# Second block's input sent to the channels unnormalised, its two norms computed beside the projections

## The reference, cut to what matters

```python
return rmsnorm(x, g_final)            # end of the first block
...
h = _rms_norm(x, g_pre_mix[l])        # start of the second
proj = h @ w_in[l]
qa, ka, va, c_q, c_kv, k_r, gate_logits = _split_cols(
    proj, [MOBA_WIDTH, MOBA_WIDTH, MOBA_WIDTH, MLA_Q_LORA, MLA_KV_LORA, MLA_ROPE, 2 * D_MODEL])
...
gates = jax.nn.sigmoid((gate_logits + b_gate[l]).astype(jnp.float32)).astype(x.dtype)
merged = gates[..., :D_MODEL] * o_a + gates[..., D_MODEL:] * o_b
x = x + _rms_norm(merged @ w_out[l], g_post_mix[l])
```

## Time and profile before

| | us |
|---|---|
| median of 3 runs | 913.61 |
| lowest, highest | 911.22, 915.33 |
| profiled execution, its own time | 917.53 |
| span of that execution | 915.7 |
| PE busy | 852.1 (93%) |
| DVE busy | 419.4 (46%) |
| ACT busy | 417.5 (46%) |
| POOL busy | 410.0 (45%) |

### The profile page before, as it was taken

One profiled execution on the slowest core, in us unless ns is written; L12 is line 12 of the kernel. 1 busy time (PEld: TensorE's weight loads), 2 busy tenths in 40 slices (PEclk: granted clock), 3 DMA queues, 4 the chain that ended last, 5 costly groups with the idle time before them and its releaser, 6 DMA issues.

```text
span 915.7 us, 14674 instructions
## 1 busy us (share of the span) xinstructions
PE 852.1 (93%) x5699; PEld 739.3 (81%) x5699; DVE 419.4 (46%) x647; ACT 417.5 (46%) x648; POOL 410.0 (45%) x197
## 2 busy tenths in 40 slices
PE   5899999979889799999999799999998799999996
PEld 3578877856567699999997687899897699999995
DVE  3556468893522623323425414544355644243334
ACT  4435313333644434444444474565754544444443
POOL 2444000000036165565563687655555455646643
PEclk9899999999899989999999999999999999999999
DMA  9674564127324256556553377444344155665651
GB/s 322 206 273 135 201 218 161 47 68 244 103 92 138 69 165 194 191 178 191 181 186 104 117 217 171 138 117 119 124 150 161 47 185 183 185 186 190 193 162 46
DMA packets 93821, 145.55 MB, mean 159 GB/s; under 512 B 15435, under 2 KB 63792, under 8 KB 93776
## 3 DMA queue, kind: packets, MB, share of 16 engines
q1 hardware_dynamic: 92896, 143.23, 50.6%
q0 software_dynamic: 848, 1.70, 0.7%
q10 hardware_dynamic: 32, 0.01, 0.0%
HBM read 143.87 MB, written 1.05 MB: 158 GB/s over the span
## 4 chain that ended last, share of the span: by engine, by line
PE 73%; DVE 12%; issue 6%; ACT 4%; POOL 3%; DMA 1%; SPq 0%; DVEq 0%; ACTq 0%; POOLq 0%
PE bank L1608 71%; POOL w_lo L592 2%; ACT w_hi L647 2%; POOL z_lo L621 1%; PE bank L1876 1%; PE bank L1693 1%; DVE h_f L1154 1%; DVE hg_kb L1246 1%; DVE hg_kf L1246 1%; DMA raw<-in_w_in 1%; DMA x<-in_x 1%; DVE w_lo L1092 1%; PE bank L2172 1%; DVE x L1564 1%; DVE merged L1530 1%
## 5 line engine op out<-in xcount | busy, mean ns | idle before, releaser
L592 POOL TENSOR_TENSOR w_lo<-raw,w_hi 128x1024 fp32r<-128x1024 f32 (+2 forms) x161 | 389.3, 2435 | 472.7 <-ACT w_hi L647 451.7
L647 ACT ACTIVATE w_hi<-raw 128x1024 fp32r<-128x1024 f32 (+1 forms) x218 | 225.8, 1044 | 226.6 <-PE bank L1608 191.9
L1092 DVE TENSOR_TENSOR w_lo<-raw,w_hi 128x1024 fp32r<-128x1024 f32 x60 | 77.2, 1295 | 145.0 <-ACT w_hi L647 144.8
L1608 PE MATMUL bank<-z_hi,w_hi 128*128 128x256 f32 x384 | 110.6, 288 | 3.5 <-POOL w_lo L592 3.2
L1608 PE MATMUL bank<-z_lo,w_hi 128*128 128x256 f32 x384 | 109.3, 285 | 0.0
L1608 PE MATMUL bank<-z_hi,w_lo 128*128 128x256 f32 x384 | 109.3, 285 | 0.0
L1608 PE MATMUL bank<-n_hi,w_hi 128*128 128x256 f32 x352 | 100.7, 286 | 4.3 <-POOL w_lo L592 3.2
L1608 PE MATMUL bank<-n_lo,w_hi 128*128 128x256 f32 x352 | 99.4, 283 | 0.0
L1608 PE MATMUL bank<-n_hi,w_lo 128*128 128x256 f32 x352 | 99.4, 282 | 0.0
L1608 PE MATMUL bank<-w_hi,mlp_h_hi 128*128 128x512 f32 x216 | 84.9, 393 | 2.9 <-DVE mlp_h_lo L1594 1.5
L1608 PE MATMUL bank<-w_lo,mlp_h_hi 128*128 128x512 f32 x216 | 84.7, 392 | 0.0
(11 more groups left out here) (369 smaller groups left out, 1667.1 us busy)
## 6 DMA issues: line engine op xcount, KB each, us to landing
raw<-in_w_in SPq DMA_DIRECT2D x54, 512.0 KB, 4.6
raw<-in_w_down SPq DMA_DIRECT2D x54, 512.0 KB, 3.6
raw<-in_w_gu SPq DMA_DIRECT2D x44, 512.0 KB, 3.5
raw<-in_w_mod SPq DMA_DIRECT2D x32, 512.0 KB, 4.4
raw<-in_w_up SPq DMA_DIRECT2D x32, 512.0 KB, 3.7
raw<-in_w_mod SPq DMA_DIRECT2D x32, 256.0 KB, 6.3
raw<-in_w_out SPq DMA_DIRECT2D x12, 512.0 KB, 3.9
raw<-in_w_in SPq DMA_DIRECT2D x8, 336.0 KB, 3.0
```

What stands on the lines that cost most here:

```text
L592: nc.gpsimd.tensor_tensor(wl[:, w % SPL, 0:size], raw[:, slot_raw, 0:size], wh[:, w % SPL, 0:size].bitcast(F32), ALU.subtract).then_inc(s_ ...
L647: nc.scalar.activation(wh[:, w % SPL, 0:size], raw[:, slot_raw, 0:size], ACT.Copy).then_inc(s_hi, 1)
L1092: V.tensor_tensor(wl[:, w % SPL, :], raw[:, slot_raw, :], wh[:, w % SPL, :].bitcast(F32), ALU.subtract).then_inc(s_lod, 1)
L1608: return nc.tensor.matmul(out_, l, r_, start=start, stop=stop, skip_group_check=True)
```

## The change

The product `g_final x g_pre_mix` per channel (`gz`) is made once at the start, for which `g_final` is also loaded as rows. `x2`, before any norm, is transposed and multiplied by `gz` alone, and ACT and DVE (no longer POOL) split it. The projections run on that. Both norms are computed beside them: `x3` as before, and the product of both factors per token, `r34`. What has tokens on the partitions gets `r34` as a scale when it leaves its bank: `qa`, `ka`, `va` on ACT, the latents and `k_r` on DVE, the squares of the latents on ACT. The gates have channels on the partitions, so they are multiplied by `rstd_b`, on DVE in place of the copy on ACT. `x2` is made in halves, banks and places in the queues change with that, the latents are transposed after `ka`, and POOL's DMAs of the post gains move behind chunk 11. `gfin` lies in another place of SBUF.

```diff
+        gz = sb("final_pre_gain", [P, 8])
...
-            pool.wait_ge(DV.sem, DV["x3 1"])
-            for j, n in enumerate(("g_post_mix_2", "g_post_mlp_2")):
-                pool.dma_start(gpost[:, j, :], a[n].broadcast_to([P, D])).then_inc(s_gp, 16)
-
...
-                if c == 2:
-                    input_lo("z")
+                if c == 12:
+                    pool.wait_ge(DV.sem, DV["x3 1"])
+                    for j, n in enumerate(("g_post_mix_2", "g_post_mlp_2")):
+                        pool.dma_start(gpost[:, j, :], a[n].broadcast_to([P, D])).then_inc(s_gp, 16)
...
-            hi2(1)
-            load_functions(LN_EXP)
-            for t in range(2):
-                act.wait_ge(DV.sem, DV[f"x2 {t}"])
-                row_norm(act, "3", t, junk)
...
+            hi2(3)
...
+            high("z", zh, zf, 0, 4)
+            hi2(4)
+            high("z", zh, zf, 4, 6)
+            hi2(5)
+            high("z", zh, zf, 6, 8)
+            hi2(6)
+            load_functions(LN_EXP)
+
+            def token_norm(name, made, scratch, chunks_):
+
+                for t in range(2):
+                    act.wait_ge(DV.sem, DV[f"{made} {t}"])
+                    if t:
+                        act.wait_ge(AC.sem, AC[f"sq {name} 0"])
+                    nc.scalar.activation(scratch, x[:, t, :], ACT.Square,
+                                         accum_out=stat[:, 64 + t:65 + t]).then_inc(AC.sem, AC.tick(f"sq {name} {t}"))
+                    hi2(chunks_[t])
+                for t in range(2):
+                    act.wait_ge(AC.sem, AC[f"sq {name} {t}"])
+                    ln_exp(act, 68 + t, 64 + t, 1, D, f"{name} {t}")
+
+            token_norm("3", "x2", junk, (7, 8))
             hi2(10)
-
+            token_norm("4", "x3", yj, (11, 12))
+            act.wait_ge(s_used, W2["latents"])
+            hi2(13)
+            act.wait_ge(DV.sem, DV["r34 1"])
+            for n, (b, w) in enumerate(((4, 384), (5, 384), (6, 256), (7, 256))):
+                if n:
+                    act.wait_ge(AC.sem, AC[f"sq5 {n - 1}"])
+                nc.scalar.activation(yj[:, 0:w], ps[b][:, 0:w], ACT.Square, scale=stat[:, 220 + n % 2:221 + n % 2],
+                                     accum_out=stat[:, 64 + n:65 + n]).then_inc(AC.sem, AC.tick(f"sq5 {n}"))
+            hi2(14)
             load_functions(LN)
...
+            act.wait_ge(AC.sem, AC["sq5 3"])
...
-                nc.scalar.activation(mqk[:, t, 0:512], ps[4 + t][:], ACT.Copy).then_inc(AC.sem, AC.tick(f"qa {t}"))
-            hi2(15)
-
+                nc.scalar.activation(mqk[:, t, 0:512], ps[t][:], ACT.Identity, scale=stat[:, 220 + t:221 + t]).then_inc(AC.sem, AC.tick(f"qa {t}"))
+            hi2(19)
+            act.wait_ge(s_used, W2["ka"])
+            for t in range(2):
+                nc.scalar.activation(mqk[:, t, 512:1024], ps[2 + t][:], ACT.Identity, scale=stat[:, 220 + t:221 + t]).then_inc(AC.sem, AC.tick(f"ka {t}"))
...
-            hi2(22)
+            hi2(23)
             act.wait_ge(s_used, W2["va"])
             for t in range(2):
-                nc.scalar.activation(va[:, t, :], ps[4 + t][:], ACT.Copy).then_inc(AC.sem, AC.tick(f"va {t}"))
+                nc.scalar.activation(va[:, t, :], ps[t][:], ACT.Identity, scale=stat[:, 220 + t:221 + t]).then_inc(AC.sem, AC.tick(f"va {t}"))
...
+            V.tensor_tensor(gz[:], cols[:, R_FIN:R_FIN + 8], cols[:, R_PRE:R_PRE + 8], ALU.mult)
...
-            dve.wait_ge(PE.sem, PE["mlp 0 1"])
             for t in range(2):
-                if t:
-                    dve.wait_ge(s_used, W0 + 6 + 12 * MLP1_TRIPS)
                 for j in range(2):
-                    ins = V.tensor_tensor(xn[:, t, 512 * j:512 * j + 512], ps[4 + 2 * t + j][:], ga2[:, 512 * j:512 * j + 512], ALU.mult)
-                done(ins, f"o2 {t}")
-                tick(V.tensor_tensor(x[:, t, :], x[:, t, :], xn[:, t, :], ALU.add), f"x2 {t}")
+                    c = slice(512 * j, 512 * j + 512)
+                    if t and j:
+                        dve.wait_ge(s_used, W0 + 6 + 12 * MLP1_TRIPS)
+                    else:
+                        dve.wait_ge(PE.sem, PE[f"mlp {t} {j}"])
+                    done(V.tensor_tensor(xn[:, t, c], ps[4 + 2 * t + j][:], ga2[:, c], ALU.mult), f"o2 {t} {j}")
+                    tick(V.tensor_tensor(x[:, t, c], x[:, t, c], xn[:, t, c], ALU.add), f"x2 {t}" if j else f"x2 {t} first")
+
+            def z_lo(k):
+                dve.wait_ge(AC.sem, AC[f"zh {k}"])
+                tick(V.tensor_tensor(zl[:, k, :], zf[:, k % 4, :], zh[:, k, :].bitcast(F32), ALU.subtract), f"zl {k}")
+
+            for k in range(KT):
+                dve.wait_ge(PE.sem, PE[f"zT {k // 2}"])
+                if k >= 2:
+                    z_lo(k - 2)
+                    own(f"zl {k - 2}")
+                tick(V.tensor_scalar(zf[:, k % 4, :], ps[k // 2][:, T * (k % 2):T * (k % 2) + T], gz[:, k:k + 1], None, ALU.mult), f"z {k}")
+            z_lo(6)
+            z_lo(7)
+
             dve.wait_ge(s_gf, 16)
             for t in range(2):
                 refine("3", t, 64 + t, lambda: dve.wait_ge(AC.sem, AC[f"sq 3 {t}"]))
-                done(V.scalar_tensor_tensor(out=x[:, t, :], in0=x[:, t, :], scalar=stat[:, 216 + t:217 + t], in1=gfin[:],
+                done(V.tensor_copy(stat[:, 218 + t:219 + t], stat[:, 216 + t:217 + t]), f"r3 {t}")
+                done(V.scalar_tensor_tensor(out=x[:, t, :], in0=x[:, t, :], scalar=stat[:, 218 + t:219 + t], in1=gfin[:],
                                             op0=ALU.mult, op1=ALU.mult), f"x3 {t}")
+            for t in range(2):
+                refine("4", t, 64 + t, lambda: dve.wait_ge(AC.sem, AC[f"sq 4 {t}"]))
+                done(V.tensor_tensor(stat[:, 220 + t:221 + t], stat[:, 218 + t:219 + t], stat[:, 216 + t:217 + t], ALU.mult), f"r34 {t}")
+                tick(V.tensor_scalar(dg[:, t, :], ident, stat[:, 220 + t:221 + t], None, ALU.mult), f"z diag {t}")
...
-            factors("4", "z")
-            channels("z", R_PRE)
-
             dve.wait_ge(AC.sem, AC["rstd 5"])
             for t in range(2):
-                V.tensor_copy(qr[:, t, 8, :], ps[2 + t][:, 256:288])
-                V.tensor_scalar(cc[:, t, 0:384], ps[t][:, 0:384], stat[:, 68 + t:69 + t], None, ALU.mult)
-                ins = V.tensor_scalar(cc[:, t, 384:640], ps[2 + t][:, 0:256], stat[:, 70 + t:71 + t], None, ALU.mult)
+                r_ = stat[:, 220 + t:221 + t]
+                V.tensor_scalar(qr[:, t, 8, :], ps[6 + t][:, 256:288], r_, None, ALU.mult)
+                V.tensor_scalar(cc[:, t, 0:384], ps[4 + t][:, 0:384], r_, stat[:, 68 + t:69 + t], ALU.mult, ALU.mult)
+                ins = V.tensor_scalar(cc[:, t, 384:640], ps[6 + t][:, 0:256], r_, stat[:, 70 + t:71 + t], ALU.mult, ALU.mult)
...
+            dve.wait_ge(PE.sem, PE["z rstd"])
+            done(V.tensor_copy(rby[:], ps[7][:, 0:T]), "z rstd")
...
+                if m % 2:
+                    g = m // 2
+                    dve.wait_ge(s_used, W2[f"gates {g}"])
+                    for j in range(2):
+                        tick(V.tensor_tensor(gates[:, 4 * g + 2 * j:4 * g + 2 * j + 2, :], ps[6 + j][:].rearrange("p (a t) -> p a t", a=2),
+                                             rby[:].unsqueeze(1).broadcast_to([P, 2, T]), ALU.mult), f"gates {g} {j}")
                 if m == 5:
                     o_lo(0)
...
-            rows_by_channel("z", "x3", ((3, 9), (3, 1), (3, 4), (3, 5)))
+            for t in range(2):
+                for j in range(2):
+                    if t:
+                        keep_clock(4, 1)
+                    pe.wait_ge(DV.sem, DV[f"x2 {t}" if j else f"x2 {t} first"])
+                    for k in range(4 * j, 4 * j + 4):
+                        c = T * (k % 2) + P * t
+                        ins = nc.tensor.transpose(ps[k // 2][:, c:c + P], x[:, t, P * k:P * k + P], ident)
+                        if t and k % 2:
+                            ins.then_inc(PE.sem, PE.tick(f"zT {k // 2}"))
+            keep_clock(4, 2)
...
+            tokens2(0)
+            tokens2(2)
...
-            tokens2(6)
+            pe.wait_ge(DV.sem, DV["z diag 1"])
+            mm(ps[7][:, 0:T], ones, dg[:].rearrange("p t k -> p (t k)"), True).then_inc(PE.sem, PE.tick("z rstd"))
```

More of the change, by code:

```diff
@@ L970, in _ @@
                 hi2(29 + 2 * m)
-                if m % 2:
-                    g = m // 2
-                    act.wait_ge(s_used, W2[f"gates {g}"])
-                    for j in range(2):
-                        nc.scalar.activation(flat(gates, 4 * g + 2 * j, 2), ps[6 + j][:], ACT.Copy).then_inc(AC.sem, AC.tick(f"gates {g} {j}"))
                 causal_probs_by_key(2 * m)
@@ L985, in _ @@
             hi2(44)
-            act.wait_ge(AC.sem, AC["gates 3 1"])
+            act.wait_ge(DV.sem, DV["gates 3 1"])
             for j in range(16):
@@ L2118, in gates_chunk @@
                 if m and m % 4 == 0:
-                    pe.wait_ge(AC.sem, AC[f"gates {m // 4 - 1} 1"])
```

(3 more changed lines are left out.)

45 lines of the change are left out of this document (12 added, 33 removed).

## The result

| | before | after |
|---|---|---|
| median, us | 915.31 (6 runs) | 921.65 (6 runs) |
| lowest to highest | 911.22 to 917.53 | 919.21 to 923.63 |
| ratio | | 1.0071, 95% interval 1.0043 to 1.0100 |
| span of the profiled execution | 915.7 | 919.8 |
| its mean granted clock | 0.978 | 0.977 |

The change costs 6.3 us. A second set of ten runs of the changed kernel gave 920.69 and the same ratio, 1.0071. I had forecast 916.0 with a range of 906.5 to 920.5: the direction is right, and the time lies 1.15 us above the range. The median of before that I started from, 913.61, was itself 1.7 us low.

The account below looks back on a forecast made before the run. TensorE, busy 93% of the span, was taken as the bound. -0.2 up to `uq`, +2.4 at `o_lo` and +0.1 for small edits make +2.3; 913.61+2.3 = 916 us, range 906.5 to 920.5.

Parts of the forecast that it names:

- edits at nothing: Small edits, among them the gain product on 8 columns and the eleventh row DMA at the start, priced at +0.1 us.
- the forecast's +2.3: Whole kernel: -0.2 up to `uq`, +2.4 at `o_lo`, +0.1 for small edits, added to the median of 913.61.
- The front: Hand-over from first MLP to second block: chunk 0 starts at 503.3 instead of 513.93, -10.6 us.
- a sign of being right: At the hand-over: first multiply from `z_hi` within 4 us of the last MLP multiply.
- The wait of 2.54 for `z_lo`: At chunk 2 of the second block: PE's wait behind POOL goes, -2.5 us, and its low clock, -1.7.
- What it gives back up to chunk 13: PE waits for late weights: +3.5 at chunks 5, 6, 8, 9; +3.3 at chunk 11; +3.2 at chunk 13.
- The race of the r step with `w_lo` 8: Norm of tile 0: if POOL is first, `x3` comes 2.4 us later; one extra `w_lo` or low clock, chance 0.22.
- The low clock: Between the hand-over and `uq`: two idle stretches over 3 us lower the clock, 1.7 us each, +3.4.
- the rival alone: At `o_lo`: the 2.5 us idle lowers the clock, 1.7 us; one extra `w_lo` or low clock, chance 0.22.
- the sum of all that: Everything up to `uq`: the 14.8 us won are given back within 60 us, -0.2 in all.
- The wait before `uq`: Copies of `va` now stand behind `w_hi` of chunk 22, so PE waits longer than today's 1.2 us, +0.7.
- `o_lo`.: Causal attention, gates 2: DVE makes the gates before `o_lo(0)`, so PE waits for head pair 4, +2.4 us.

Follow-up runs that it names:

- before_shift: The kernel before with an unused tile of 64 bytes per partition, so later tiles stand where the changed kernel has them; median 917.70 us, ratio 1.0042.
- after_again: The changed kernel run once more, unaltered, ten runs; median 920.69 us, ratio 1.0071 to the kernel before.

## Why the prediction was wrong, point by point

**The step that failed is "edits at nothing".** It named the gain product's 8 columns and the eleventh row's DMA and priced what they do, not where they stand. Their place costs 3.8 us by before_shift (0.42%, interval 0.19 to 0.65), the low clock in it included. With that, the forecast's +2.3 would have been +6.1, against 6.3 measured. That the two agree to 0.2 is luck, since the 3.8 alone is uncertain by 2 us. At equal places the change costs 2.7 us by the ratios at 64 bytes (1.0071 against 1.0042) and 6.7 at 128 (1.0040 against 0.9967); by the medians 3.0 and 3.9. Each of these has an uncertainty of some 3 us, and my 2.3 is just below the lowest. So what the change costs without its shift isn't known closer than these four figures, 2.7 to 6.7.

**The front.** -10.6 forecast, -9.7 measured. I had put down the half sum of `x` at 0.61, and not seen that it meets the two early `w_lo` and takes 1.91. The first multiply on `z` came 4.5 us after the last one of the MLP, and I had named 4 as a sign of being right. The wait of 2.54 for `z_lo` went as forecast; its low clock, seen in one trace of four at 1.55, is worth some 0.4 on average, not 1.7.

**What it gives back up to chunk 13.** +3.5, +3.3 and +3.2 forecast, 2.1 (0.81 at chunk 5, 1.03 at 6, 0.25 at 8, none at 9), 2.18 and 4.40 measured: 10.0 against 8.7. The mechanism, DVE's two-input steps held by POOL and the chunks behind them on ACT, was right. The race of the r step with `w_lo` 8, which I had as a rival, went the other way (519.22 against 519.14), so `x3` of tile 0 came at 524.96 instead of 522.0 and held chunk 10, not 11. POOL then had nothing to do for 3.3 us, in which all steps of tile 1 got through, so chunk 11 was in time.

**The low clock.** I had put down two stretches in this part at 1.7 each. There were one or two, and the second cost nothing, since 68.5 us passed with one as with two. The ones that cost are behind `o_lo`, which I had in the rival alone: 3.4 in the first trace, 0 in the second.

**Between the last product and `uq`** the sum of all that was -0.2. It was -0.3 against the first trace of before, +1.3 against the second, which has no low stretch, and +0.4 against before_shift (68.11), which has none either and the tiles at the same place. The wait before `uq` grew from 1.22 to 2.19, by 0.97, forecast 0.7. That the sum came out so well is luck, since errors cancel in it: 1.0 less was won (the front, and 1.55 for 1.7), and 0.9 went by the pace (68.11 against 67.24), but the waits and the low stretch gave back 3.3 less (8.7 and at most 1.4, against 10.0 and 3.4). Some 1 us stays unexplained.

**`o_lo`.** +2.4 forecast, +2.25 measured (2.41 against 0.16), and +2.35 for the whole stretch from `uq` to the first multiply on `o_hi` against before_shift (89.86 in after_again, 87.51).

**The base.** The median of three runs was 913.61; over the later groups of runs it is 914.1 to 916.4. One profiled execution is as uncertain: the two of before have spans of 915.7 and 910.0, and between them and the changed kernel's 919.8 any cost from 4 to 10 could be read. A part of that scatter lies ahead of the first MLP, where no wait was looked at: its first multiply starts at 302.0 to 304.2 in the four traces of the kernel before, with and without an unused tile, and at 302.4 to 305.8 in the ten of the changed one and its variants. Whether the change costs something there stays open.

## What to carry to other kernels

When work moves beside GpSimd, look at the inputs that each VectorE step takes from SBUF before you look at its columns: beside POOL a step on one column took 2.33, where 0.16 is its time, and one on 1024 took 3.18, where 1.28 is. With the second factor written as a scalar operand the one column steps took 0.15 to 0.28 beside POOL. It is no rule for all steps with one input: the 128 column diagonal took 2.30 and 2.40, where 0.29 is its time. A new small tile near the start of SBUF moves every operand behind it. Before a difference under 1% is put down to a mechanism, compare the pace of an untouched stretch in both traces, and run the old kernel with the same shift.
